# A block of constant matmuls in the stream's form, at 16 operand distances, ahead of a two-block forward pass

## The chip, the cores and the metric

One core of one Trainium2 chip. The metric is the time of one execution on the device, in microseconds (us); lower is better. The inputs are fp32, and so is the output.

## What is computed

The reference runs a sequence of 256 positions of width 1024 through two model blocks of two layers each. Cut to what matters for the work here:

```python
def first_block(x, ...):            # 2 layers
    h = rmsnorm(x, norm_mix_pre[l]); proj = h @ w_in[l]
    # retention, short convolution, 31-tap convolution, three gated branches
    x = x + rmsnorm(merged @ w_o[l], norm_mix_post[l])
    h = rmsnorm(x, norm_ffn_pre[l]); up = causal_dwconv(h @ w_up[l], ffn_conv_w[l])
    x = x + rmsnorm((silu(gate) * val) @ w_down[l], norm_ffn_post[l])

def second_block(x, ...):           # 2 layers
    z = rms(x) @ w_in_2             # mLSTM, sparse attention, differential attention, gates
    x = x + merged @ w_out_2
    x = x + (silu(g) * u) @ w_down_2
```

Nearly all the arithmetic is x times a weight matrix, and every weight is read once.

## The kernel before

The host lays all weight matrices out as one stream of 582 pieces. A piece is 128 partitions x 1024 columns of fp32, 512 KB, eight blocks of 128 x 128, in the order in which TensorE uses them. The activations stand transposed, channels on partitions and the 256 positions along the free dimension.

**A piece's way.** SyncE loads piece j into F[:, j % 5] (`piece`, L2585). ScalarE rounds it to fp32r into H, the high part (`high_part`, L1871). VectorE writes F - H into L, the low part (`low_part`, L1094, its instruction at L1097). The activations are split in the same way, HH and HL (FH and FL for the branch and feed-forward inputs). For every block `channel_blocks` gives TensorE three matmuls of 128 x 256 into one PSUM bank of big: high x high, high weight x low activation, low weight x high activation. Below they are called a triple. All matmuls go through one helper, L582, where the weight (stationary) operand is lhsT and the moving operand is rhs. For v and a few other projections `token_blocks` exchanges the roles: the activation is stationary, and 512 columns of weights move.

```python
mm(ps, hi, xh, start=(k == 0), stop=False)
mm(ps, hi, xl, start=False, stop=False)
r = mm(ps, lo, xh, start=False, stop=last)
```

**Buffers.** F, H and L hold five pieces each. SyncE loads piece j when `low_part` of piece j - 5 is done (s_lo), and ScalarE and VectorE fill H and L of piece j when TensorE has used piece j - 5 (s_mm). They lie in SBUF in the order of their declaration: F, H, L, X, "apart" (48 fp32 columns, 192 bytes, used by nothing), HH, HL, FH, FL, and after them parameters, constants and a pool of tiles called POOL. FHa and FLa are the names of FH and FL as tensors of 14 x 256 columns.

**The order of work.** Each engine has a program of its own, written out as one queue, and semaphores tie them. `tensor_program` walks the groups of the stream. Ahead of the first group it calls `norm(0)`: column sums of the squares of X (L581, helper `column_sums`), a few matmuls of constants to keep the engine busy (`keep_busy`), a matmul with a matrix of ones that spreads the factors over the partitions, and then the first group, four channel groups woven, 32 blocks or four pieces. `norm(0)` on VectorE adds the squares (L1138), forms the factors (L1141 to L1127), prepares the low part of piece 0 and then writes X times factor (L1218) and the low parts of it (L1232); on ScalarE it squares X (L1890), rounds piece 0 (L1874), takes the root (L1867) and rounds the eight tiles to HH (L1907), with the high parts of pieces 1 to 3 between them. VectorE's and GpSimd's queues begin with memsets: two of one element on VectorE (L1815, L1816; ScalarE's first activation waits for the second), four on GpSimd (L2559 to L2562).

**PSUM.** There are eight banks, big0 to big3 for the stream and small0 to small3 for everything else. `norm(0)` uses small0, small2 and small3.

Of the kernel before, what the change touches and what calls it, by code (L numbers as in the profile page):

```python
# [7 lines left out]
F32 = mybir.dt.float32  # L8
# [4 lines left out]
P = 128  # L13
T = 256
# [248 lines left out]
def two_blocks_kernel(nc, stream, params, consts, decay, turn2, lam_rows, xT, head_rows, out):  # L263
# [9 lines left out]
    with ctx:  # L273
        def sb(name, shape, dt=F32):
            return ctx.enter_context(nc.sbuf_tensor(name, shape, dt))

        def sem(name):
            return ctx.enter_context(nc.semaphore(name))

        F = sb("F", [P, NF, PB * P])  # L280
        H = sb("H", [P, NR, PB * P], F32R)
        L = sb("L", [P, NR, PB * P], F32R)
# [4 lines left out]
        FHa = sb("FH", [P, 14, T], F32R)  # L287
        FLa = sb("FL", [P, 14, T], F32R)
# [9 lines left out]
        small = [ctx.enter_context(nc.psum_tensor(f"small{i}", [P, 512], F32)) for i in range(4)]  # L298
# [7 lines left out]
        def tile(i, n=1):  # L306
            return POOL[:, i * T:(i + n) * T]
# [43 lines left out]
        SQ, SK, SV, DQ, DK, DV_, HSQ = 33, 37, 29, 8, 12, 59, 45  # L351
# [42 lines left out]
        s_f = [sem(f"s_f{i}") for i in range(NF)]  # L394
        s_x, s_x2, s_ones, s_par, s_const, s_turn = (sem(n) for n in ("s_x", "s_x2", "s_ones", "s_par", "s_const", "s_turn"))
        s_dec, s_lam, s_out, s_eps, s_pad = (sem(n) for n in ("s_dec", "s_lam", "s_out", "s_eps", "s_pad"))
        s_hi, s_lo, s_mm = sem("s_hi"), sem("s_lo"), sem("s_mm")
        s_eva, s_evd = sem("s_eva"), sem("s_evd")
        s_fill = [sem(f"s_fill{i}") for i in range(4)]
# [120 lines left out]
        def fresh(n):  # L520

            if n == 0 or G[n].layer != G[n - 1].layer:
                return True, 2 * G[n].layer
            if G[n].named("fg"):
                return True, 2 * G[n].layer + 1
            return G[n].named("out") or G[n].named("down"), None
# [34 lines left out]
        def needed(g):  # L561

            m = g.members[0]
            if m.j or m.label not in ("y0", "y1", "y2", "s_k"):
                return []
            if not m.second:
                return {"y0": ["retention"], "y2": ["long_conv"]}.get(m.label, [])
            return {"y0": ["mrows", "mlstm"], "y1": ["choice", *(f"head_{name}" for name in NAMES), "sparse0", "sparse1"],
                    "y2": ["diff0", "diff1"], "s_k": ["ckv"]}[m.label]


        def tensor_program(pe):
# [89 lines left out]
            def channel_blocks(g):  # L662

                n = len(g.members)
                banks_ = [bank_for(m) for m in g.members]
                for i in range(g.nblocks):
                    if i == middle(g):
                        yield
                    k, m, ps = i // n, g.members[i % n], banks_[i % n][:, 0:T]
                    j, o = divmod(g.pos + i, PB)  # L670
                    pe.wait_ge(s_lo, j + 1)
                    hi, lo = H[:, j % NR, o * P:(o + 1) * P], L[:, j % NR, o * P:(o + 1) * P]
                    xh, xl = x_of(m, k)
                    last = k == m.nk - 1
                    wait_x(m, k, False)
                    mm(ps, hi, xh, start=(k == 0), stop=False)
                    wait_x(m, k, True)
                    mm(ps, hi, xl, start=False, stop=False)
                    r = mm(ps, lo, xh, start=False, stop=last)
                    if last or o == PB - 1:  # L680
                        r.then_inc(s_mm, 1)
# [23 lines left out]
            def norm(b):  # L705
                if b == 0:
                    pe.wait_ge(s_ones, 16)
                    bank = use(0, b, "yy")
                    pe.wait_ge(bnd_v.sem, bnd_v.at(b, "add", 0, 6))
                    column_sums(bank, 0, 1, tile(YSQ), True, False)  # L710
                    pe.wait_ge(bnd_v.sem, bnd_v.at(b, "add", 0, 7))
                    column_sums(bank, 0, 1, tile(YSQ + 1), False, True).then_inc(s_fill[0], 1)
                keep_busy(3, 2 if b in SUMMED else 3)
                pe.wait_ge(bnd_v.sem, bnd_v.at(b, "dg"))
                bank = use(2, b, "s1")
                mm(bank[:, 0:T], ones, tile(DG)).then_inc(s_fill[2], 1)
                if b not in SUMMED:
                    keep_busy(3, 4)
                    return
                keep_busy(3, 4)  # L720
                pe.wait_ge(bnd_v.sem, bnd_v.at(b, "dg2"))
                bank = use(3, b, "s2")
                mm(bank[:, 0:T], ones, tile(DG + 1)).then_inc(s_fill[3], 1)
                keep_busy(1, 4)
# [250 lines left out]
            def diff(l, t):  # L975
# [43 lines left out]
                for h in range(4):  # L1019
# [3 lines left out]
                    if h % 2:  # L1023
                        yield

            TASKS = {"retention": retention, "long_conv": long_conv, "choice": choice, "mrows": mrows,
                     "mlstm": mlstm, "ckv": ckv}
            slow = [False]
# [4 lines left out]
            def settle(n):  # L1033

                older = staged.tasks
                staged.tasks = []
                for m in G[n].members:
                    slow[0] = m.label[0:2] == "sc"
                    if m.label == "i_k":
                        staged.begin(m.label, token_weights(m))  # L1040
                    elif m.label in ("out", "down"):
                        staged.begin(m.label, squares(m))
                    for name in begun(m):
                        if name[:-1] in ("sparse", "diff"):
                            beside.add(name, (sparse if name[0] == "s" else diff)(m.l, int(name[-1])))
                        elif name[:5] == "head_":
                            beside.add(name, head(m.l, name[5:]))
                        else:
                            beside.add(name, TASKS[name](m.l))
                newer = staged.tasks  # L1050
                staged.tasks = older
                staged.step()
                staged.tasks += newer

            for n, g in enumerate(G):
                made_after, b = fresh(n)
                if made_after:
                    if n:
                        settle(n - 1)
                    staged.flush()  # L1060
                    if g.layer != G[n - 1].layer:
                        ready.clear()
                    if b is not None:
                        norm(b)
                for name in needed(g):
                    beside.finish(name)
                for _ in token_blocks(g) if g.kind == "t" else channel_blocks(g):
                    if not made_after:
                        settle(n - 1)
                    if paced(n):  # L1070
                        beside.step()
# [5 lines left out]
        def vector_program(dve):  # L1077
            beside, staged = Steps(), Steps()
            v = dve.e
# [12 lines left out]

            def low_part(j):
                dve.wait_ge(s_hi, j + 1)  # L1094
                if j >= NR:
                    dve.wait_ge(s_mm, piece_done[j - NR])
                v.tensor_tensor(L[:, j % NR, :], F[:, j % NF, :], H[:, j % NR, :].bitcast(F32),  # L1097
                                ALU.subtract).then_inc(s_lo, 1)
# [619 lines left out]
            def diff(l, t):  # L1718
# [52 lines left out]
                for k in (2, 3):  # L1771
                    low_branch(2, 2 + l, k, tile(DO + k))

            TASKS = {"retention": retention, "long_conv": long_conv, "choice": choice, "mrows": mrows,
                     "mlstm": mlstm, "ckv": ckv}
# [4 lines left out]
            def settle(n, low=0):  # L1780

                for m in G[n].members:
# [24 lines left out]
                    for name in begun(m):  # L1807
# [4 lines left out]
                        else:  # L1812
                            beside.add(name, TASKS[name](m.l))

            v.memset(eps, EPS)  # L1815
            v.memset(eps64, 64 * EPS).then_inc(s_eps, 1)  # L1816
            for n, g in enumerate(G):
# [33 lines left out]
        def scalar_program(act):  # L1851
# [17 lines left out]

            def high_part(j):  # L1870
                act.wait_ge(s_f[j % NF], 16 * (j // NF + 1))  # L1871
                if j >= NR:
                    act.wait_ge(s_mm, piece_done[j - NR])
                a.activation(H[:, j % NR, :], F[:, j % NF, :], ACT.Copy).then_inc(s_hi, 1)  # L1874
# [451 lines left out]
            def rows_out(l, t, u):  # L2326
# [3 lines left out]

            TASKS = {"retention": retention, "long_conv": long_conv, "choice": choice, "mrows": mrows,
                     "mlstm": mlstm, "ckv": ckv}
# [6 lines left out]
            def settle(n):  # L2339

                for m in G[n].members:
# [27 lines left out]
                    for name in begun(m):  # L2369
# [4 lines left out]
                        else:  # L2374
                            beside.add(name, TASKS[name](m.l))

# [29 lines left out]
        def pool_program(gp):  # L2406
            beside, staged = Steps(), Steps()
            q = gp.e
# [130 lines left out]

            TASKS = {"retention": retention, "long_conv": long_conv, "choice": choice, "mlstm": mlstm, "ckv": ckv}  # L2540

            def settle(n):

                for m in G[n].members:
# [10 lines left out]
                    for name in begun(m):  # L2555
                        if name in TASKS:
                            beside.add(name, TASKS[name](m.l))

            q.memset(glu[:, :, 0:30], 0.0).then_inc(s_pad, 1)  # L2559
            q.memset(tile(CX, 2)[:, 0:2], 0.0).then_inc(s_pad, 1)  # L2560
            q.memset(tile(ROWS), 0.0)
# [245 lines left out]
```

## Time and profile before

| | |
|---|---|
| median of 2 runs | 1868.96 us (1867.89 and 1870.03) |
| profiled execution, from its first to its last instruction | 1870.4 us |
| TensorE busy in it | 1811.5 us, 97% |
| VectorE busy | 1364.4 us, 73% |
| ScalarE busy | 1076.2 us, 58% |
| GpSimd busy | 187.5 us, 10% |
| DMA | 320.08 MB, mean 171 GB/s |

The profiled execution has no time beside its span of its own; the two runs stand for what lies around it, and their median is 1.4 us below that span.

Engines in the rows: PE is TensorE's matmuls, PEld its weight loads, DVE VectorE, ACT ScalarE, POOL GpSimd, SP SyncE. A number such as L582 is a line of the kernel. Matmuls are pipelined and their ends are modelled, so neighbours overlap in the rows: how fast they go is read from the distance between starts. A matmul on plain fp32 operands has two records. PEclk is the clock granted to TensorE, 1.00 being the full one.

### The profile page before, as it was taken

How to read it: one execution, taken by the hardware profiler on the slowest of the kernel's cores; microseconds unless marked ns; L12 is line 12 of the kernel's file. 1: busy time of each engine (PE TensorE's matmuls, PEld its weight loads, DVE VectorE, ACT ScalarE, POOL GpSimd, SP SyncE). 2: the span in 40 equal slices, each digit the busy share in tenths (PEclk: the TensorE clock that was granted, in tenths of full speed). 3: DMA queues.
4: the chain of work that ended last, by engine and by line, in shares of the span. 5: the costliest groups of instructions: out<-in, count | busy, mean ns of one | idle time of the engine just before them, and what ended most of it. 6: DMA issues, size and time to landing. Idle time of an engine off the chain costs nothing.

```text
span 1870.4 us, 36335 instructions
## 1 busy us (share of the span) xinstructions
PE 1811.5 (97%) x14784; PEld 1768.1 (95%) x14784; DVE 1364.4 (73%) x2385; ACT 1076.2 (58%) x1812; POOL 187.5 (10%) x200
## 2 busy tenths in 40 slices
PE   8999999999999999999999999999998999999998
PEld 8899999999899999999889888999998998899998
DVE  6897789867889789866767767655558587676553
ACT  5455656655355666654676685545455757755542
POOL 1012410001003410001111003000002010030000
PEclk9999999999999999999999999999998999999999
DMA  7445536564545536554445644566554375355553
GB/s 283 168 152 187 185 124 203 193 206 155 187 148 180 181 128 200 189 196 135 155 137 167 196 136 129 181 197 193 194 160 140 126 200 160 128 170 180 194 195 108
DMA packets 90342, 320.08 MB, mean 171 GB/s; under 512 B 10528, under 2 KB 12992, under 8 KB 90048
## 3 DMA queue, kind: packets, MB, share of 16 engines
q1 hardware_dynamic: 90176, 317.75, 52.2%
q8 instruction: 118, 1.93, 0.4%
q14 instruction: 48, 0.39, 0.1%
HBM read 310.60 MB, written 1.08 MB: 167 GB/s over the span
## 4 chain that ended last, share of the span: by engine, by line
PE 78%; DVE 11%; ACT 5%; issue 3%; POOL 1%; DMA 1%; SPq 0%; DVEq 0%; ACTq 0%; POOLq 0%
PE big L582 71%; PE small L582 5%; DVE L L1097 3%; PE small L581 2%; DVE POOL L1454 2%; ACT H L1874 2%; DVE POOL L1324 1%; DMA POOL<-POOL 1%; POOL POOL L2470 1%; ACT POOL L2258 1%; DVE gates L1341 0%; DVE POOL L1286 0%; ACT POOL L2296 0%; POOL POOL L2449 0%; SPq L2613 0%
## 5 line engine op out<-in xcount | busy, mean ns | idle before, releaser
L582 PE MATMUL big<-HH,H 128*128 128x256 f32 x3344 | 950.1, 284 | 6.2 <-DVE gates L1341 3.5
L582 PE MATMUL big<-HL,H 128*128 128x256 f32 x3344 | 933.7, 279 | 3.8 <-DVE HL L1232 3.6
L582 PE MATMUL big<-HH,L 128*128 128x256 f32 x3344 | 932.6, 279 | 0.0
L1097 DVE TENSOR_TENSOR L<-F,H 128x1024 fp32r<-128x1024 f32 x574 | 702.4, 1232 | 196.4 <-ACT H L1874 195.0
L1874 ACT ACTIVATE H<-F 128x1024 fp32r<-128x1024 f32 x582 | 610.3, 1054 | 207.5 <-PE big L582 204.4
L582 PEld LDWEIGHTS big<-HH,H 128*128 128x128 f32 x3344 | 634.8, 190 | 11.2 <-DVE gates L1341 4.2
L582 PEld LDWEIGHTS big<-HL,H 128*128 128x128 f32 x3344 | 633.5, 189 | 7.8 <-DVE HL L1232 5.4
L582 PEld LDWEIGHTS big<-HH,L 128*128 128x128 f32 x3344 | 632.6, 189 | 0.0
L582 PE MATMUL big<-FH,H 128*128 128x256 f32 x848 | 240.1, 283 | 0.0
L582 PE MATMUL big<-FL,H 128*128 128x256 f32 x848 | 236.2, 278 | 0.0
L582 PE MATMUL big<-FH,L 128*128 128x256 f32 x848 | 236.1, 278 | 0.0
L582 PEld LDWEIGHTS big<-FH,H 128*128 128x128 f32 x848 | 160.8, 190 | 1.1 <-issue 1.0
L582 PEld LDWEIGHTS big<-FL,H 128*128 128x128 f32 x848 | 159.4, 188 | 1.1 <-issue 1.0
L582 PEld LDWEIGHTS big<-FH,L 128*128 128x128 f32 x848 | 159.3, 188 | 0.0
L582 PE MATMUL small<-POOL 128*128 128x128 f32 (+2 forms) x352 | 82.9, 356 | 26.0 <-DVE POOL L1414 6.8
L1454 DVE SCALAR_TENSOR_TENSOR POOL<-POOL,PR 128x256 f32<-128x256 f32 x240 | 103.9, 496 | 0.1
L582 PE MATMUL big<-ffn,H 128*128 128x256 f32 x512 | 89.2, 277 | 0.0
L582 PEld LDWEIGHTS small<-POOL 128*128 128x128 f32 x352 | 54.1, 194 | 33.6 <-issue 7.7
L582 PEld LDWEIGHTS big<-ffn,H 128*128 128x128 f32 x512 | 77.4, 188 | 0.0
L582 PE MATMUL big<-ffn,L 128*128 128x256 f32 x256 | 71.0, 277 | 0.0
L1355 DVE SCALAR_TENSOR_TENSOR POOL<-big,PR,POOL 128x255 f32<-128x255 f32 x88 | 42.3, 481 | 25.3 <-ACT POOL L2052 20.9
L2449 POOL TENSOR_TENSOR POOL<-POOL,gates 128x256 f32<-128x256 f32 x32 | 30.4, 973 | 266.5 <-DVE gates L1341 266.5
(238 smaller groups left out, 1805.7 us busy)
## 6 DMA issues: line engine op xcount, KB each, us to landing
F<-in_stream SPq DMA_DIRECT2D x582, 512.0 KB, 3.8
POOL<-POOL SPq DMA_DIRECT2D x32, 128.0 KB, 4.2
POOL<-head_rows SPq DMA_DIRECT2D x8, 256.0 KB, 5.0
X<-in_x SPq DMA_DIRECT2D x2, 512.0 KB, 4.4
POOL<-POOL SPq DMA_DIRECT2D x16, 64.0 KB, 3.2
out_x<-X SPq DMA_DIRECT2D x1, 1024.0 KB, 3.9
POOL<-in_decay SPq DMA_DIRECT2D x1, 768.0 KB, 10.9
POOL<-POOL SPq DMA_DIRECT2D x8, 96.0 KB, 5.1
```

What stands on the lines that cost most here:

```text
L581: return pe.e.matmul(out_, lhsT, rhs, start=start, stop=stop, skip_group_check=True)
L582: return pe.e.matmul(out_, lhsT, rhs, start=start, stop=stop)
L1097: v.tensor_tensor(L[:, j % NR, :], F[:, j % NF, :], H[:, j % NR, :].bitcast(F32), ALU.subtract).then_inc(s_lo, 1)
L1324: r = v.scalar_tensor_tensor(out=acc[:, d:T], in0=ps[:, 0:T - d], scalar=par("2m_w", l, (3 - d) * 8 + c), in1=acc[:, d:T], op0=ALU.mult, o ...
L1355: v.scalar_tensor_tensor(out=dst[:, 1:T], in0=ps[:, 0:T - 1], scalar=par("ffn_w", l, 44 + row), in1=dst[:, 1:T], op0=ALU.mult, op1=ALU.add ...
L1454: r = v.scalar_tensor_tensor(out=acc, in0=glu[:, j, k:k + T], scalar=par("cf_w", l, k * 4 + j), in1=acc, op0=ALU.mult, op1=ALU.add)
L1874: a.activation(H[:, j % NR, :], F[:, j % NF, :], ACT.Copy).then_inc(s_hi, 1)
L2258: r = a.activation(p[:, e * nk:(e + 1) * nk], p[:, e * nk:(e + 1) * nk], ACT.Exp, bias=mx[:, e:e + 1], scale=root_of_queries("s_q", qt, pa ...
L2449: q.tensor_tensor(home, home, gate_tile(b, m.j), ALU.add).then_inc(mrg_g.sem, mrg_g.up(m.layer, b, m.j))
L2470: q.tensor_tensor(tile(dst), tile(x), tile(y), ALU.add).then_inc(lc_g.sem, lc_g.up(l, event))
```

## The change

TensorE's queue gets a new function, `warm()`, ahead of the first group's norm. It waits for five memsets (three new ones at the head of VectorE's queue, two at the head of GpSimd's) that fill H and L of slots 3 and 4, one tile of POOL, FH and FL with constants. Then it issues 34 runs of six triples into small2: for 16 starts of the moving operand, 16 bytes apart, the weights being at fixed places, once behind an fp32 matmul of 128 x 256 and once behind an fp32r matmul of 128 x 512 (`pushed`, into small3), and twice more with the order of the triple's last two exchanged. Two runs of six 512-wide matmuls with a 256-wide one behind each (`wide`) close it. No result of these is read. ScalarE's and VectorE's work on piece 3 waits for the block's last matmul (s_warmed), since it overwrites slot 3. Nothing else is changed.

```diff
+        s_warm, s_warmed = sem("s_warm"), sem("s_warmed")
...
+            def warm():
+
+                pe.wait_ge(s_warm, 5)
+                xs, ys = FHa[:, :, :].rearrange("p k n -> p (k n)"), FLa[:, :, :].rearrange("p k n -> p (k n)")
+
+                def pushed(kind):
+                    if kind == 0:
+                        mm(small[3][:, 0:T], tile(HSQ)[:, 0:P], tile(HSQ))
+                    else:
+                        mm(small[3][:, :], H[:, 3, 0:P], H[:, 4, 0:512])
+
+                def triples(n, at, order):
+                    r = None
+                    for k in range(n):
+                        hi, lo = H[:, 3 + k // 8, (k % 8) * P:(k % 8 + 1) * P], L[:, 3 + k // 8, (k % 8) * P:(k % 8 + 1) * P]
+                        xh, xl = xs[:, at + T * k:at + T * (k + 1)], ys[:, at + T * k:at + T * (k + 1)]
+                        turns = ((hi, xh), (hi, xl), (lo, xh)) if order == 0 else ((hi, xh), (lo, xh), (hi, xl))
+                        for i, (w, x) in enumerate(turns):
+                            r = mm(small[2][:, 0:T], w, x, start=(k == 0 and i == 0), stop=(k == n - 1 and i == 2))
+                    return r
+
+                def wide(n, at):
+                    for k in range(n):
+                        hi, lo = H[:, 3, k * P:(k + 1) * P], L[:, 3, k * P:(k + 1) * P]
+                        mm(small[2][:, :], hi, xs[:, at + 512 * k:at + 512 * (k + 1)])
+                        r = mm(small[3][:, 0:T], lo, xs[:, at + 512 * k:at + 512 * k + T])
+                    return r
+
+                for kind in range(2):
+                    for d in range(0, 256, 16):
+                        pushed(kind)
+                        triples(6, (64 + d) % 256 // 4, 0)
+                for kind in range(2):
+                    pushed(kind)
+                    triples(6, 0, 1)
+                    pushed(kind)
+                    r = wide(6, 0)
+                r.then_inc(s_warmed, 1)
...
+            warm()
             for n, g in enumerate(G):
...
             def low_part(j):
                 dve.wait_ge(s_hi, j + 1)
+                if j == 3:
+                    dve.wait_ge(s_warmed, 1)
...
+            v.memset(H[:, 3:5, :].bitcast(F32), 0.5).then_inc(s_warm, 1)
+            v.memset(tile(HSQ), 0.5).then_inc(s_warm, 1)
+            v.memset(FHa[:, :, :].bitcast(F32), 0.75).then_inc(s_warm, 1)
             v.memset(eps, EPS)
             v.memset(eps64, 64 * EPS).then_inc(s_eps, 1)
...
             def high_part(j):
                 act.wait_ge(s_f[j % NF], 16 * (j // NF + 1))
+                if j == 3:
+                    act.wait_ge(s_warmed, 1)
...
+            q.memset(L[:, 3:5, :].bitcast(F32), 0.25).then_inc(s_warm, 1)
+            q.memset(FLa[:, :, :].bitcast(F32), 0.75).then_inc(s_warm, 1)
             q.memset(glu[:, :, 0:30], 0.0).then_inc(s_pad, 1)
```

TensorE's queue before begins with the norm's column sums; small and big are PSUM banks, CO the constants, the names in brackets are semaphores:

```order
L581 MATMUL small<-CO,POOL 128x1 [waits norm_dve,s_ones]
L581 MATMUL small<-CO,POOL 128x1
L581 MATMUL small<-CO,POOL 128x1 [waits norm_dve]
L581 MATMUL small<-CO,POOL 128x1
L582 MATMUL small<-CO 128x128 x3
L582 MATMUL small<-POOL,CO 128x256 [waits norm_dve]
L582 MATMUL small<-CO 128x128 x4
L582 MATMUL big<-HH,H 128x256 [waits x_high,s_lo]
```

In the changed kernel the same queue begins with the block, whose first push waits for s_warm:

```order
L583 MATMUL small<-POOL 128x256 [waits s_warm]
L583 MATMUL small<-FH,H 128x256
L583 MATMUL small<-FL,H 128x256
L583 MATMUL small<-FH,L 128x256
L583 MATMUL small<-FH,H 128x256
```

and goes over from it to the norm, 672 instructions later, thus:

```order
L583 MATMUL small<-FH,H 128x512
L583 MATMUL small<-FH,L 128x256
L582 MATMUL small<-CO,POOL 128x1 [waits norm_dve,s_ones]
L582 MATMUL small<-CO,POOL 128x1
L582 MATMUL small<-CO,POOL 128x1 [waits norm_dve]
L582 MATMUL small<-CO,POOL 128x1
L583 MATMUL small<-CO 128x128 x3
L583 MATMUL small<-POOL,CO 128x256 [waits norm_dve]
L583 MATMUL small<-CO 128x128 x4
L583 MATMUL big<-HH,H 128x256 [waits x_high,s_lo]
```

The norm and the first group stand behind the block in unchanged order, one line number further on.

VectorE's queue in the changed kernel, at its head (SCR holds single columns, eps among them):

```order
L1858 MEMSET H 128x2048
L1859 MEMSET POOL 128x256
L1860 MEMSET FH 128x3584
L1861 MEMSET SCR 128x1
L1862 MEMSET SCR 128x1
L1181 TENSOR_TENSOR POOL<-POOL 128x256 [waits norm_act] x2
```

The three large memsets have come ahead of the two that were there, and of the adds.

## Rows read from the trace of the kernel before

**Rows 1.** The page: busy time by engine, and the chain that ended last

```profile
PE 1811.5 (97%) x14784; PEld 1768.1 (95%) x14784; DVE 1364.4 (73%) x2385; ACT 1076.2 (58%) x1812; POOL 187.5 (10%) x200
...
PE 78%; DVE 11%; ACT 5%; issue 3%; POOL 1%; DMA 1%; SPq 0%; DVEq 0%; ACTq 0%; POOLq 0%
```

**Rows 2.** Timeline of the head: start, length, engine, line, operation, out<-in

```profile
0.87 0.06 DVE L1815 MEMSET SCR<- 128x1 f32 x1 [0.87 <-PEq L2799]
1.21 3.52 POOL L2562 MEMSET POOL<- 128x4096 f32 x1
4.79 2.58 ACT L1890 ACTIVATE POOL<-X 128x256 f32<-128x256 f32 x8 [2.50 <-DMA X<-in_x]
7.76 1.84 PE L581 MATMUL small<-CO,POOL 128*128 128x1 f32 x8 [7.76 <-DVE POOL L1138]
9.46 1.63 PE L582 MATMUL small<-CO 128*128 128x128 f32 x6
10.33 0.42 DVE L1127 TENSOR_TENSOR POOL<-CO,SCR 128x256 f32<-128x256 f32 x1
10.88 1.15 PE L582 MATMUL small<-POOL,CO 128*128 128x256 f32 x2
11.82 1.92 PE L582 MATMUL small<-CO 128*128 128x128 f32 x8
12.07 0.87 DVE L1218 SCALAR_TENSOR_TENSOR POOL<-X,PR,small 128x256 f32<-128x256 f32 x2 [0.18 <-PE small L582]
13.39 0.48 PE L582 MATMUL big<-HH,H 128*128 128x256 f32 x1
13.71 0.28 PE L582 MATMUL big<-HL,H 128*128 128x256 f32 x1
```

**Rows 3.** The chain that ended last, in order of time, in the head

```profile
0.80 3.97 DMA X<-in_x
...
7.76 1.84 PE small L581 x8
...
14.37 1.23 DVE L L1097
...
22.10 0.34 DVE HL L1232
22.44 0.04 issue
22.48 13.79 PE big L582 x119
```

**Rows 4.** Timeline of TensorE in the first group; 17 matmuls lie between the two

```profile
13.95 0.28 PE L582 MATMUL big<-HH,H 128*128 128x256 f32 x1
...
15.99 0.28 PE L582 MATMUL big<-HH,H 128*128 128x256 f32 x1
```

**Rows 5.** The same in a later stretch; 14 matmuls lie between the two

```profile
123.94 0.28 PE L582 MATMUL big<-HH,H 128*128 128x256 f32 x1
...
125.70 0.28 PE L582 MATMUL big<-HH,H 128*128 128x256 f32 x1
```

**Rows 6.** TensorE: 512-wide matmuls, three between the two; then an fp32 pair in the stream

```profile
46.98 0.39 PE L582 MATMUL big<-H,HH 128*128 128x512 f32 x1
...
47.90 0.39 PE L582 MATMUL big<-H,HL 128*128 128x512 f32 x1
...
82.24 0.59 PE L582 MATMUL small<-POOL,CO 128*128 128x256 f32 x2
...
82.90 0.28 PE L582 MATMUL big<-HH,L 128*128 128x256 f32 x1
```

**Rows 7.** TensorE: column sums at a later norm

```profile
242.42 1.39 PE L581 MATMUL small<-CO,POOL 128*128 128x1 f32 x12
```

**Rows 8.** Stretches: length, busy us of each engine, PEclk, DMA share, GB/s

```profile
251.00:256.00 5.00, 3.83 (x22) 3.33 (x22) 4.68 (x13) 1.25 (x4) 2.09 (x3) 0.84 0.31 105
280.00:300.00 20.00, 20.00 (x179) 20.00 (x178) 19.53 (x33) 14.12 (x26) 0.00 (x0) 1.00 0.66 217
```

**Rows 9.** Groups of instructions: the stream's matmuls and their weight loads, busy us, mean ns

```profile
L582 PE MATMUL big<-HH,H 128*128 128x256 f32 x3344 | 950.1, 284 | 6.2 <-DVE gates L1341 3.5
L582 PEld LDWEIGHTS big<-HL,H 128*128 128x128 f32 x3344 | 633.5, 189 | 7.8 <-DVE HL L1232 5.4
```

**Rows 10.** DMA issues: KB each and us from issue to landing

```profile
F<-in_stream SPq DMA_DIRECT2D x582, 512.0 KB, 3.8
```

## The prediction

> **What bounds the kernel now.** I read first the busy shares and the chain that ended last [rows 1]: TensorE is busy 1811.5 of 1870.4 us, 97%, and stands for 78% of the chain. So TensorE's queue is the clock of this kernel, and 1870.4 - 1811.5 = 58.9 us is all that it does not fill. Work put into that queue costs its own length, unless it falls into one of those gaps. Next I read the head in the timeline [rows 2], since the change stands there: TensorE does nothing until 7.76 us, where the column sums of the first norm begin, and the first weight matmul is at 13.39. The chain [rows 3] says what that head hangs on: the load of X, the squares, the sums, and then VectorE and ScalarE, which make the pieces until 22.44; only from 22.48 is it TensorE alone. Last I read the distance from one start to the next in the stream [rows 4 to 6], because a matmul's own duration (284 ns in the mean [rows 9]) overlaps the next and can't be multiplied by a count.
>
> **What the change adds.** warm() stands ahead of norm(0) in TensorE's queue and waits for five memsets. Its count, from the loops: 32 rounds of one push and 6 triples, two more rounds of that kind, and two rounds of one push and 6 pairs of wide and narrow. That is 34 x 18 = 612 matmuls of 128x256 in fp32r, 18 pushes of 128x256 in fp32 (two records each), 18 pushes of 128x512 in fp32r, and 12 x (512 + 256) columns, 672 instructions in all. It moves nothing else; queued behind it on TensorE is everything, and VectorE and ScalarE wait for the norm's sums as before.
>
> **Start of the block.** No VectorE memset of any size is in the trace; the two there are of one element, 0.06 us. The nearest: VectorE's tensor_tensor takes 0.42 us for 256 elements and 1.23 for 1024 [rows 2, 3], so (1.23 - 0.42) / 768 = 1.055 ns an element with 0.15 us fixed. The three memsets write 2048 + 256 + 3584 = 5888 elements: 6.2 us, from 0.87 to about 7.2, and the first push starts near 7.3. Bounds: at GpSimd's rate for a memset, 3.52 us for 4096 [rows 2], it would be 5.1 us and the start near 6.0; at the full 1.23 / 1024 an element 7.1 us and the start near 8.1. I take the slope, since it is this engine's. GpSimd's own two, 5632 elements, take 4.8 us by its row and end near 5.7, so they lie under VectorE's. The eps memset stands behind on VectorE and ScalarE's first activation waits for it, so ScalarE's eight squares (2.6 us) run from about 7.3 to 10; that and VectorE's adds lie under the block and cost nothing. GpSimd's old memset of 4096 ends about 5 us later, also under it.
>
> **Length of the block at the full clock.** The stream starts its 128x256 matmuls 18 in 2.04 us, 0.113 us each, in one stretch [rows 4], and 15 in 1.76 us, 0.117 us each, in another [rows 5]. Stretches of both kinds follow small matmuls in this trace, so I take the middle with a little weight on the slower, 0.1158: 612 x 0.1158 = 70.9 us (bounds 69.2 and 71.8). The wide ones start 0.92 / 4 = 0.23 us apart [rows 6], so 18 x 0.23 = 4.1, and the twelve pairs 12 x (0.23 + 0.115) = 4.1. An fp32 push: from its start at 82.24 to the third matmul behind it at 82.90 is 0.66 us, less two spacings of 0.115 is 0.43 [rows 6]; 18 x 0.43 = 7.8. Together 86.9 us.
>
> **The clock at its start.** The granted clock reads 1.00 over the head, but the durations don't: the same fp32 128x256 pair takes 1.15 us at 10.88 and 0.59 at 82.24, and the pushes of identity columns at 9.46 and 11.82 are as slow [rows 2, 6]. So TensorE ran at 1.2 of its two levels, 1.2 and 2.4 GHz, from its first work at 7.76 until somewhere between 12.03, when that pair ended, and 13.71, the first matmul of 0.28 us. That is 4.3 to 6.0 us after it began to work. The block will begin at the low level too; 5 us at half speed lose 2.5 us (bounds 1.7 and 3.0, and since the slow work of before was sparser, I let it go down to 1.5).
>
> **What comes back.** When the block ends, the clock is high for the norm, and everything it waits for is there. The eight records of column sums took 1.84 us [rows 2]; at the high level twelve take 1.39 [rows 7], so eight take about 1.0: 0.8 back. The sum over all partitions, 1.15 to 0.59: 0.55 back. The rest, from VectorE's first 128x256 at 12.07 to 22.44, is its and ScalarE's chain, equally long after the block: no more comes back, and the small waits of TensorE inside it stay.
>
> **Sum.** 7.3 + 86.9 + 2.5 = 96.7 us is where the column sums begin, against 7.76: +88.9. Less 1.35 is +87.6. The profiled span of 1870.4 becomes 1958.0. The span stands 1.4 us above the median of the two runs, 1868.96, so I predict 1956.6 us. A change under 2%, 37.4 us, counts as none for this kernel.
>
> **Later stages.** Nothing in them is edited. The five pieces in F are loaded while the block runs, yet the pieces behind them need s_lo(0), which comes after the block, and the piece rate is set by TensorE. What can differ is the clock: it falls at the norms and the attention heads, as between 251.0 and 256.0 with 0.84 [rows 8]. Those falls begin at moments that don't belong to the kernel, so 88 us later some will be longer and some shorter; the two runs of before lie 2.1 us apart, and I allow 3 us either way. One of them may now fall on norm(0), since TensorE works thinly there: up to 1.7 us.
>
> **Rival: the distances matter.** The block puts the moving operand at 16 starts, 16 bytes apart, against weights that stand still. In the stream it stands at one of them only, as the declarations have it: H, L and X are multiples of 256 bytes, "apart" adds 192, and HH, HL, FH and FL follow. The token matmuls have the roles exchanged, so 64, and their 512 columns go at 0.23, no slower than two of 256. What speaks for a penalty elsewhere is only that two spacings exist and that a weight load of 189 ns [rows 9] lies beside each matmul of 0.115 spacing, so both operands are read at once. Price: where load and matmul no longer overlap, the spacing can go up to 0.189 + 0.113 = 0.30 us; a distance at which it is bound by the load alone gives 0.189, 0.073 more. If half of the 576 triples' matmuls in the sweep paid that, 288 x 0.073 = 21 us: 1977.6. If a quarter did, 1967. The Trainium skill speaks against it ("TensorE: Matmul & The Clock Gate", step by step, on LDWEIGHTS): the engine has two independent read ports, and loading the next weights takes nothing from the running matmul. By that rule all 16 distances cost alike and the sum above stands; this trace agrees at 192 and 64 and shows no other, and it does show two spacings, which the rule has no name for. Chance of a penalty over 6 us: 0.12.
>
> **Rival: all in the fast spacing, or the memsets quick.** With 0.113 throughout, the block at 6.0 and 1.5 us for the low clock it comes to 6.0 + 85.3 + 1.5 - 7.76 - 1.35 = +83.7: 1952.7. Chance 0.15, inside the range.
>
> **Rival on the other side: the lead pays the block.** Were the stream late because its pieces are late, then a start with F full would take gaps away. Its price: all of the 58.9 us that TensorE does not fill, less the 7.8 of the head, 51.1 us; +87.6 - 51.1 = +36.5, 1905.5, which is not slower by 2%. It decides only if the lead is kept to the end and every gap is a wait for pieces. Against it: a piece of 512 KB lands in 3.8 us [rows 10] and five are in flight, TensorE takes 24 x 0.115 = 2.8 us for one, and the long stretches run without a gap [rows 8]; also the pieces' high parts 3 and up wait for the block, so the lead is five loaded pieces and no more. Chance 0.01.
>
> **Does it do what it says?** If the memsets did not hold TensorE up, or the block lay beside loads that the head waits for, its cost would shrink by at most the 7.76 us of idle head, and that is already in the sum.
>
> **How the numbers follow.** The sum as it stands has 0.72, the fast variant 0.15, the penalty 0.12, the lead 0.01. Terms: start -1.3 to +0.8, spacing -1.7 to +0.9, low clock -1.0 to +0.5, later clock 3 either way, norm(0) up to +1.7. They don't all add on one side, so 1951; above I reach into the penalty case, to 1967. All but the last case lie above 2%: faster 0.005, same 0.015, slower 0.98.
>
> **What would show it.** Right: the first push near 7.3 us, spacings of 0.226 falling to 0.113 to 0.118 some 5 us later, the block's end at 96 to 97, the first matmul on HH and H about 4.3 us behind it, and the stream's groups with the means of before. Wrong: a round of the sweep longer than the others by over 1 us (the distance rival), a first push before 6.5 or after 8.2, or TensorE's idle time without the head far from 51 us.

## The result, and the profile after

| | kernel before | changed kernel |
|---|---|---|
| first measurement | 1868.96 us, 2 runs | 1956.9 us, 2 runs (1950.53 and 1963.27) |
| ratio | | 1.0471, 95% interval 1.0419 to 1.0523 |
| measured again beside the before (e9) | 1869.3 us, 11 runs | 1959.26 us, 6 runs, ratio 1.0471 (1.0427 to 1.0514) |
| profiled execution | span 1870.4 us | 1950.53 us, span 1948.8 us |

Slower by 4.7%, as forecast. The page of the changed kernel has, for [rows 1]:

```profile
PE 1892.5 (97%) x15474; PEld 1845.9 (95%) x15474; DVE 1369.3 (70%) x2388; ACT 1075.8 (55%) x1812; POOL 192.5 (10%) x202
...
PE 80%; DVE 10%; ACT 5%; issue 2%; POOL 1%; DMA 1%; SPq 0%; DVEq 0%; ACTq 0%; POOLq 0%
```

TensorE has 81 us more of busy time, 690 more records (672 instructions, 18 of them with two), and is still 97% busy. Its idle time is 1948.8 - 1892.5 = 56.3 us against 58.9. Without the wait ahead of the first instruction that is 49.2 against 51.1, so next to nothing of the block fell into gaps behind the head.

The head, for [rows 2]; the timeline's columns are start, length, engine, line, operation:

```profile
1.30 1.76 DVE L1858 MEMSET H<- 128x2048 f32 x1 [1.30 <-PEq L2849]
3.06 0.27 DVE L1859 MEMSET POOL<- 128x256 f32 x1
4.03 3.04 DVE L1860 MEMSET FH<- 128x3584 f32 x1 [0.69 <-issue]
7.13 1.22 PE L583 MATMUL small<-POOL 128*128 128x256 f32 x2 [7.13 <-DVE FH L1860]
...
97.15 0.95 PE L582 MATMUL small<-CO,POOL 128*128 128x1 f32 x8
...
99.30 0.70 PE L583 MATMUL small<-POOL,CO 128*128 128x256 f32 x2 [0.43 <-DVE POOL L1170]
...
100.30 0.87 DVE L1261 SCALAR_TENSOR_TENSOR POOL<-X,PR,small 128x256 f32<-128x256 f32 x2
```

The block stands between 7.13 and 97.15, 90.0 us. VectorE's first product of X and the factors, the point from which the head is VectorE's and ScalarE's chain, has moved from 12.07 to 100.30: +88.2 us. What is left to the end took 1848.5 us instead of 1858.3.

What the block itself tells: its rounds. Each begins with a push, so the difference of two pushes is a round of 18 matmuls. Behind the 512-wide push, in the timeline of TensorE:

```profile
61.56 0.39 PE L583 MATMUL small<-H 128*128 128x512 f32 x1
...
63.95 0.39 PE L583 MATMUL small<-H 128*128 128x512 f32 x1
...
66.34 0.39 PE L583 MATMUL small<-H 128*128 128x512 f32 x1
...
68.66 0.39 PE L583 MATMUL small<-H 128*128 128x512 f32 x1
...
71.02 0.39 PE L583 MATMUL small<-H 128*128 128x512 f32 x1
...
73.29 0.39 PE L583 MATMUL small<-H 128*128 128x512 f32 x1
```

These are the rounds at 80 (2.39 us), 96 (2.39), 112 (2.32), 128 (2.36) and 144 (2.27). At 144 every start is 113 or 114 ns behind the one before, from the first; at 112 so from the tenth; at 80 it goes 117, 124, 117, 122 and on, at 96 116, 123, 119, 121 and on, 120 in the mean at both. At 192, the stream's own distance, the round behind the 512-wide push reached 113 after five matmuls, and the one behind the fp32 push stayed at 117 to 119 through all 18. Once settled, all the other rounds at the full clock lie between 116.3 and 120.2 in the mean. So there is a close spacing of 113.3 ns, and there are several wide ones of up to 120; both spacings that the stream showed [rows 4, 5] occur at one and the same distance.

### The profile page after: what moved, and what is told of

Read it like the earlier page. It is cut to its first block, busy times and chain, and to the rows that moved or that the text cites. A ratio compares the mean times of both kernels' runs of the same rounds, so it can differ in the third digit from the quotient of the medians.

```text
span 1948.8 us, 37722 instructions
## 1 busy us (share of the span) xinstructions
PE 1892.5 (97%) x15474; PEld 1845.9 (95%) x15474; DVE 1369.3 (70%) x2388; ACT 1075.8 (55%) x1812; POOL 192.5 (10%) x202
## 4 chain that ended last, share of the span: by engine, by line
PE 80%; DVE 10%; ACT 5%; issue 2%; POOL 1%; DMA 1%; SPq 0%; DVEq 0%; ACTq 0%; POOLq 0%
PE big L583 69%; PE small L583 9%; DVE L L1140 2%; PE small L582 1%; ACT H L1922 1%; DVE POOL L1497 1%; DMA POOL<-POOL 1%; DVE POOL L1367 1%; POOL POOL L2518 1%; ACT POOL L2306 1%; SPq L2663 0%; DVE gates L1384 0%; ACT POOL L2344 0%; PE small L586 0%; POOL POOL L2497 0%
## 5 line engine op out<-in xcount | busy, mean ns | idle before, releaser
L583 PE MATMUL small<-POOL 128*128 128x128 f32 (+2 forms) x388 | 92.9, 356 | 28.1 <-DVE FH L1860 7.1
L583 PEld LDWEIGHTS small<-POOL 128*128 128x128 f32 x388 | 58.9, 191 | 35.6 <-DVE FL L1740 7.3
L583 PE MATMUL small<-FH,H 128*128 128x256 f32 (+1 forms) x216 | 65.6, 306 | 0.0
```

What stands on the lines that cost most here:

```text
L583: return pe.e.matmul(out_, lhsT, rhs, start=start, stop=stop)
```

## Experiments

The kernel before was run beside each group: 19 times with e1 to e4 (median 1872.55 us, 1857.87 to 1884.77), 11 times with e5 to e7 (1873.59), 11 times with e9 and e10 (1869.3). Two questions were open: does the block cost its length and nothing else, and what are the two spacings of the stream?

**e1, the block without its matmuls.** All matmuls but one triple are left out of warm(); the outputs don't depend on it.

```diff
-                for kind in range(2):
-                    for d in range(0, 256, 16):
-                        pushed(kind)
-                        triples(6, (64 + d) % 256 // 4, 0)
...
+                r = triples(1, 0, 0)
                 r.then_inc(s_warmed, 1)
```

> The changed kernel with the block cut to three matmuls (one triple); the five memsets, their waits and the waits on s_warmed stay. Theory (the block costs its own length on TensorE and nothing else): what is left is the delay of VectorE's eps memset, for which ScalarE's squares wait; the squares end about 2.5 us later than before, so 1869 + 2.5 = 1871.5 us, between 1868 and 1875. Rival (the new memsets and waits carry a fixed cost of their own, or the seven more us of lead bring gaps back): outside 1866 to 1876.

Measured: 1868.46 us in 12 runs, ratio 0.9998 (0.9961 to 1.0035). The timeline of its head has the delay that the memsets leave:

```profile
7.14 0.20 ACT L2418 ACTIVATE SCR<-SCR 128x1 f32<-128x1 f32 x1 [5.06 <-DVE SCR L1854]
7.25 2.54 ACT L1930 ACTIVATE POOL<-X 128x256 f32<-128x256 f32 x8
...
10.21 1.84 PE L582 MATMUL small<-CO,POOL 128*128 128x1 f32 x8 [2.07 <-DVE POOL L1173]
```

The column sums begin 2.45 us later than in [rows 2], the 2.5 expected; that is inside the scatter of the runs, so only the profile shows it. Any other cost of the memsets and waits is too small to tell from the runs, whose interval is 0.4%, some 7 us, to either side.

**e2, half the sweep.** The 16 rounds behind the fp32 push are left out.

```diff
-                for kind in range(2):
+                for kind in range(1, 2):
                     for d in range(0, 256, 16):
```

> The changed kernel with the sweep behind the fp32 push left out (16 of the 34 runs of triples); the sweep behind the 512-wide push and the tail stay. Theory (additive): the 16 rounds took 42.6 us in the profile, 1.7 of which is the low clock at the start, which the next rounds inherit, so 40.9 us come back: 1957 - 41 = 1916 us, within 6 us. Rival (part of the cost of the block is fixed, or given back later, because the long dense block changes where the clock falls): more than 8 us off.

Measured: 1918.51 us in 6 runs, ratio 1.0254 (1.0204 to 1.0305). Against 1872.55 the remaining half costs 46 us; 88 - 41 = 47 was due. The cost is additive. Its first rounds:

```profile
7.13 0.79 PE L583 MATMUL small<-H 128*128 128x512 f32 x1 [7.13 <-DVE FH L1860]
...
11.56 0.63 PE L583 MATMUL small<-H 128*128 128x512 f32 x1
...
14.69 0.39 PE L583 MATMUL small<-H 128*128 128x512 f32 x1
```

4.43 and 3.13 us for what takes 2.38 and 2.37 in the changed kernel: here the low clock cost 2.8 us, against 1.7 in the changed kernel's profile (first round 4.25, second 2.57). It is not the missing rounds that do it: e9's profile, of the changed kernel itself, has 4.86 and 3.01 us for the same two, 2.7 us lost. The length of the low clock changes from execution to execution.

**e3, the stream at 112.** No block. HH, HL, FH, FL, ffn and gates are moved so that all the stream's moving operands stand 112 bytes (mod 256) past their weights.

```diff
+        def shifted(name, shape, dt=F32):
+            flat = sb(name, [shape[0], shape[1] * shape[2] + 64], dt)
+            return flat[:, 4:4 + shape[1] * shape[2]].rearrange("p (k n) -> p k n", k=shape[1])
...
-        sb("apart", [P, 48])
-        HH = sb("HH", [P, KT, T], F32R)
-        HL = sb("HL", [P, KT, T], F32R)
+        sb("apart", [P, 24])
+        HH = shifted("HH", [P, KT, T], F32R)
+        HL = shifted("HL", [P, KT, T], F32R)
```

FH, FL, ffn and gates go the same way.

> No block. The kernel before with HH, HL, FH, FL, ffn and gates moved so that every 128x256 matmul of the stream has its moving operand 112 bytes (mod 256) past its weights instead of 192. Theory (the distance decides whether a stretch falls into the spacing of 113 ns): in the sweep the round at 112 reached 113 ns after six matmuls behind both pushes, so the 5,100 stream matmuls that stand at 118 ns drop to 113: about 22 us, 1847 us, and no less than 10 us. Rival (the slow stretches are set by what stands between the matmuls, not by the distance): 1869 within 4 us, and the same 5,100 at 118 ns. Third: 112 locks in only late, and is slower in between: 1869 to 1880.

Measured: 1853.21 us in 8 runs, ratio 0.99 (0.9865 to 0.9935): 1% faster than the kernel before. Of the stream's 13,344 matmuls of 128x256, counted by the distance to the next start, 11,793 stand at 112 to 114 ns and 1,274 at 115 to 129, where the kernel before has 7,953 and 5,109; the rest have a pause behind them. That is 3,835 wide spacings fewer, x 4.5 ns = 17 us, an estimate from one execution of each; the medians differ by 19. e10, with the same layout, has 11,746. The theory was right in its kind and a little too large in its size (22): behind an interruption the stream at 112 needs up to some 15 matmuls before it is at 113.

The spread shrank as well. The eight runs lie between 1847.44 and 1856.37, those of the kernel before between 1857.87 and 1884.77.

**e4, the same distance by the weights.** H and L move by 16 bytes, apart is 128.

```diff
-        H = sb("H", [P, NR, PB * P], F32R)
-        L = sb("L", [P, NR, PB * P], F32R)
+        H = shifted("H", [P, NR, PB * P], F32R)
+        L = shifted("L", [P, NR, PB * P], F32R)
...
-        sb("apart", [P, 48])
+        sb("apart", [P, 32])
```

> No block. The kernel before with H and L moved by 16 bytes and apart made 128 bytes, so that the distance is again 112 mod 256, but the weights and not the moving operand stand off a 32-byte line. Theory (only the distance counts): the same time as the run with the activations moved, within 3 us. Rival (the moving operand's own place counts): 1869 within 4 us whatever the other gives.

Measured: 1914.06 us in 6 runs, ratio 1.0228 (1.0179 to 1.0277). Neither was right: 60 us slower than e3 at the same distance. Only 51 matmuls of the stream stand at 113, the others at 119.6 in the mean. The same stretch as in [rows 8], TensorE only, in e3 and in e4:

```profile
280.00:300.00 20.00, 20.00 (x179) 1.00 0.62 212
```

```profile
280.00:300.00 20.00, 20.00 (x169) 1.00 0.60 201
```

The clock is 1.00 and TensorE 100% busy in both, and yet one gets 179 matmuls done and the other 169: the busy share shows nothing of this, the count does. So the distance is no full description. The buffers' own addresses in the program say where e4 differs: the weights start 16 bytes off a multiple of 32 there, and on one in the kernel before and in e3.

**e5, the stream at 144.** As e3, with apart at 32 columns.

```diff
-        sb("apart", [P, 24])
+        sb("apart", [P, 32])
```

> No block. As the run with the activations at 112, but at 144. In the sweep the round at 144 stood at 113 ns from its first matmul behind the 512-wide push and never reached it (116 to 118) behind the fp32 push. Theory (what stands ahead of a stretch and the distance together decide): stretches behind fp32 matmuls, which are most of the interruptions here, stay at 116 to 118, those behind 512-wide ones at 113; so no gain over 112, and 1860 to 1873 us. Rival (the distance alone decides, and 144 had the shortest round of all): 1850 or less, all at 113.

Measured: 1898.86 us in 6 runs, ratio 1.0142 (1.0107 to 1.0176). The rival falls, and the theory was too kind: 18 matmuls of the stream are at 113, everything else at 118.3 in the mean. The single round of the sweep that stood at 113 at this distance says that the close spacing exists there, not that the stream gets into it.

**e6, long rounds.** 40 triples in a round instead of 6, the operands used over and over, no tail; the outputs don't depend on it.

```diff
-                        hi, lo = H[:, 3 + k // 8, (k % 8) * P:(k % 8 + 1) * P], L[:, 3 + k // 8, (k % 8) * P:(k % 8 + 1) * P]
-                        xh, xl = xs[:, at + T * k:at + T * (k + 1)], ys[:, at + T * k:at + T * (k + 1)]
+                        hi, lo = H[:, 3, (k % 6) * P:(k % 6 + 1) * P], L[:, 3, (k % 6) * P:(k % 6 + 1) * P]
+                        xh, xl = xs[:, at + T * (k % 12):at + T * (k % 12 + 1)], ys[:, at + T * (k % 12):at + T * (k % 12 + 1)]
...
-                        triples(6, (64 + d) % 256 // 4, 0)
+                        r = triples(40, (64 + d) % 256 // 4, 0)
```

> The changed kernel with 40 triples in each of the 32 rounds (six weights and twelve moving tiles used over and over) and no tail. Theory (a stretch at an unfavourable distance never leaves its slow spacing by itself): rounds at 112 and 192 reach 113 ns within some ten matmuls, the others repeat their pattern of 116 to 124 ns for all 120; the kernel takes about 1872 + 3840 x 0.1175 + 16 x 0.43 + 16 x 0.23 = 2334 us. Rival (every stretch reaches 113 in the end, six triples were only too short): all rounds at 113 ns in their last half.

Measured: 2344.72 us in one run. The pushes at 112, 128, and the end of that round, then those at 192 and 208:

```profile
111.65 0.59 PE L583 MATMUL small<-POOL 128*128 128x256 f32 x2
...
125.72 0.59 PE L583 MATMUL small<-POOL 128*128 128x256 f32 x2
...
140.55 0.60 PE L583 MATMUL small<-POOL 128*128 128x256 f32 x2
...
184.23 0.59 PE L583 MATMUL small<-POOL 128*128 128x256 f32 x2
...
198.29 0.59 PE L583 MATMUL small<-POOL 128*128 128x256 f32 x2
```

14.07 us at 112, 14.83 at 128, 14.06 at 192. The last 60 starts of each round are 113.3 ns apart at 112 and 192 behind both pushes, and 116.7 to 120.0 at all other distances. A round that is still wide after its first 18 matmuls stays wide for all 120, and the stream says the same of far longer stretches: in the twelve profiles none changes its spacing later than some 17 matmuls after an interruption, and the longest has 1,582. 144 was wide behind both pushes this time, and 192 close behind both, though it had stayed wide behind the fp32 push in the changed kernel: the first 18 matmuls of a round have the same addresses in both kernels, so at those two distances the same push leads into either spacing, by what ran ahead of it.

**e7, the weights swept.** The moving operand stays at the stream's place, the weights move by 0 to 240 bytes, no tail.

```diff
-                        hi, lo = H[:, 3 + k // 8, (k % 8) * P:(k % 8 + 1) * P], L[:, 3 + k // 8, (k % 8) * P:(k % 8 + 1) * P]
+                        c = 3 * PB * P + off + P * k
+                        hi, lo = hf[:, c:c + P], lf[:, c:c + P]
...
-                        triples(6, (64 + d) % 256 // 4, 0)
+                        r = triples(6, (192 - d) % 256 // 4, 0)
```

> The changed kernel with the moving operand left where the stream has it (192) and the weights moved by 0 to 240 bytes in steps of 16, so that the distances are the same 16, in the same order; no tail. Theory (only the distance counts): each round as long as the one of the same distance in the changed kernel, within 15 ns. Rival (the weights' own place counts beside it: they read slower off a 32-byte line, as the stream at 112 by its weights suggests): the eight odd multiples of 16 stand near 119.6 ns a matmul, 40 ns or more a round above their fellows, the eight even ones equal the changed kernel's rounds.

Measured: 1951.66 us in one run. The eight distances at which the weights start on a multiple of 32 repeat the changed kernel's rounds within 1 ns a matmul at 0, 64, 96 and 224 and within 3 at 32, 128 and 160; 192 is wide behind both pushes, where the changed kernel had it close behind one. Of the eight others none is close. The telling one is 112, close behind both pushes in the changed kernel and 120 behind both here:

```profile
26.85 0.59 PE L583 MATMUL small<-POOL 128*128 128x256 f32 x2
...
29.44 0.59 PE L583 MATMUL small<-POOL 128*128 128x256 f32 x2
```

2.59 us for that round against 2.51 in the changed kernel. "Only the distance counts" falls; the rival's plain 119.6 for all eight is too simple too: they go from 117 to 121, and at 48 and 208 they are shorter than the changed kernel's rounds (2.53 against 2.56 us at 48 behind the fp32 push). In e4 and here only the weights stand off a multiple of 32, the moving operand being on one; both off together was not run.

**e8, a grid.** Weights at 0, 32, ... 224, and for each the moving operand at its 16 places, behind an fp32 push, 14 triples each.

```diff
+                for w in range(0, 256, 32):
+                    for d in range(0, 256, 16):
+                        pushed(0)
+                        r = triples(14, w // 4, (64 + d) % 256 // 4)
```

> The changed kernel with its block replaced by 128 rounds, an fp32 push and 14 triples each: weights moved by 0, 32, ... 224 bytes, and for each of these the moving operand at the 16 places of the sweep. Theory (where the weights stand off a multiple of 32 bytes they only read slower, else the distance counts): for each of the eight places the rounds that end at 113 ns are those whose distance is 112 or 192, so the pattern moves on by two rounds with each step of the weights. Rival (each operand's own place counts, so the distance is no description at all): the rounds at 113 ns are at other distances for other places of the weights, or only where the weights start on a multiple of 128 or 256 bytes. Time: 128 x (0.43 + 42 x 0.118) = 689 us on top of 1872, 2561 us, 20 less or more by how many of them lock.

Measured: 2556.27 us in one run. Mean distance of the last 19 starts of a round, where it was 113.3:

```
weights moved by   0    32    64    96   128   160   192   224
at distance 112   yes   yes   yes   yes   yes   yes   yes   yes
at distance 192   yes   yes   no    yes   yes   yes   yes   yes
elsewhere          -     -     -     -     -    64     -     -
```

The other 112 rounds lie between 116.4 and 120.1. The pushes around the first round of the weights at 64 (distance 192) and around their round at 112, in the timeline:

```profile
181.43 0.59 PE L583 MATMUL small<-POOL 128*128 128x256 f32 x2
...
186.81 0.59 PE L583 MATMUL small<-POOL 128*128 128x256 f32 x2
```

```profile
240.85 0.59 PE L583 MATMUL small<-POOL 128*128 128x256 f32 x2
...
246.10 0.59 PE L583 MATMUL small<-POOL 128*128 128x256 f32 x2
```

5.38 us where it stayed wide, 5.25 where it became close. The rounds at 113.3 move on with the weights, so with weights on a multiple of 32 bytes it is the distance that counts, and the rival of each operand's own place falls. The theory misses one round at 64, and one at 192 that stayed wide; its other half, that weights off such a multiple only read slower, has no round here, and e7 speaks against it.

**e9 and e10, the price once more.** e9 is the changed kernel, e10 the changed kernel with the layout of e3, the block's starts chosen so that its 16 distances are kept.

```diff
-                        triples(6, (64 + d) % 256 // 4, 0)
+                        triples(6, (144 + d) % 256 // 4, 0)
```

> The changed kernel itself, more often, since it has only two runs so far. Theory (the block costs 88.3 us at the full clock and 1.7 for the low clock, less 0.5 for the earlier start and 1.35 in the norm, +88.2 us): ratio 1.047 against the kernel before, 1960 us where that has its median of 1872.5, with the same spread of some 12 us to either side. Rival (the 1957 of the two runs is low because the block spares later falls of the clock): 1952 or less.

> The changed kernel with the activations moved so that the stream stands at 112; the block's own 16 distances are kept by other starts. Theory: the two effects add, 1853 + 88 = 1941 us, and the spread is as small as that of the stream at 112 (within 6 us), so this is the sharper measure of the block's price. Rival (the block leaves TensorE in a state that the stream at 112 profits from or suffers under): more than 5 us off 1941.

Measured: 1959.26 us in 6 runs (1946.77 to 1967.79), ratio 1.0471 (1.0427 to 1.0514), and 1943.98 us in 6 runs (1938.49 to 1946.62), ratio 1.0383 (1.0344 to 1.0421). The effects add: e10 less e3 is 90.8 us, 2.6 more than the theory's 88.2, which two medians of different groups can't tell from it. The rival for e9 falls: no saving in the later stages shows.

## Why the prediction was right

1956.6 us was forecast, 1956.9 measured, 1959.26 in the repeat. The mechanism holds: the block costs its own length on TensorE (e1 and e2), less what the norm gives back. That the median came within 0.3 us is luck: it is that of two runs 12.7 us apart, and the medians of e9 and of e10 less e3 put the cost at 90.0 and 90.8 us, not 87.6. Step by step, by the profile:

- **Start of the block.** 7.3 us forecast, 7.13 measured. From 0.87, where VectorE's first instruction stood before, to 7.07, where the third memset ends, is 6.2 us for 5888 elements, 1.05 ns each: the slope of tensor_tensor was right, without the fixed 0.15 us of each instruction, which the sum left out. The memset rows alone would say 0.86 ns (1.76 us for 2048, 3.04 for 3584), but ahead of these two VectorE stands idle for 0.43 us longer than before and for 0.69 us with nothing that it waits for, and not ahead of the one of 256, at 0.27 us. From 0.87 to the end of the first, and from the end of the second to that of the third, it is 1.07 and 1.04 ns an element. So the rows of the two long memsets most likely begin late; the trace can't prove it.
- **Length.** 86.9 us at the full clock; 90.0 less 1.7 is 88.3. The count was right. The spacing was mis-sized: 116.3 to 120.2 at most of the 16 distances, some 118 over the block, where 115.8, the stream's mixture, was taken; 612 x 2.2 ns is the 1.4 us.
- **The low clock at the start.** 2.5 us forecast, 1.7 in this profile, 2.8 in e2's and 2.7 in e9's.
- **The norm behind it.** The stretch from the column sums to the first product took 3.15 us instead of 4.31: 1.16 back, 1.35 forecast. The clock did not fall there.
- **Together** 88.2 us at the first product, 87.6 forecast: -0.2 for the start, +1.4 for the spacing, -0.8 for the clock, +0.2 for the norm. In e9's profile the product stands at 101.33, +89.3.
- **Later stages.** The profiled run was 9.8 us shorter behind that point than the one of before, more than the 3 allowed. The mean granted clock is 0.992 of 1948.8 us, so 15.6 us were lost, against 0.988 of 1870.4, 22.4 us: up to 7 of the 9.8 are the clock's falls. The two profiles' streams are otherwise alike, 8,031 matmuls at the close spacing and 7,953. e9's runs show that it was this execution and not the change.

The distance rival was wrong in its size: distances do matter, by up to 120.0 - 113.3 = 6.7 ns a matmul, 4 us over the whole block, and not 73 ns. The Trainium skill ("TensorE: Matmul & The Clock Gate", step by step) says that the weight load does not take read bandwidth from the running matmul. The sweep shows a cost that this rule has no place for, 113.3 against 120.0 ns for the same instructions with the moving operand 16 bytes further on (112 and 128, behind the fp32 push); whether it is the reads that collide is not shown. The variant with all of the block at 113 was wrong too, and so was the lead that pays the block: the idle time behind the head went from 51.1 to 49.2 us, not to nothing.

The range was too narrow, and for the wrong reason. It took the scatter of two runs, 2.1 us, and the kernel before scatters over 27 us in all its 44 runs; of the changed kernel's eight runs three lie outside 1951 to 1967. The profiles show where the scatter comes from: in the eight profiles with the stream at 192, 4,009 (e6), 4,249 (e2), 5,801 (e7), 7,374 (e8), 7,953 (before), 8,031 (after), 9,372 (e1) and 9,609 (e9) matmuls are at the close spacing, and at 4.5 ns each the 5,600 between the ends make 25 us. From the first matmul of the stream to the end these profiles take 1866.6 us (e6) to 1841.8 (e1), and the line through the eight falls by 4.3 ns for each further matmul at the close spacing. e2's profiled run, with 4,249, was the slowest of its six, 1929.26 us, and those of e1 and e9 the fastest of theirs. Where a layout leaves no choice, the runs lie closer together: 9 us at 112 (e3), 8 in e10, and 5 and 7.5 in e4 and e5, where all of the stream is wide.

Most of the lot falls in few places. Three stretches of the stream have 1,487, 1,487 and 1,582 matmuls without an interruption, and each is close or wide as a whole once it has settled, worth some 7 us: all close in e1 and e9, two of them wide in e2, e6 and e7, one wide in the others. The first of them, in the changed kernel's two profiles (after, then e9), TensorE only:

```profile
380.00:400.00 20.00, 20.00 (x172) 1.00 0.58 188
```

```profile
380.00:400.00 20.00, 20.00 (x179) 1.00 0.65 210
```

In the block, where TensorE waits for no other engine, these same two executions agree within a nanosecond in every spacing of every round from the sixth on. So the choice at 192 repeats with the same past of TensorE alone, and in the stream something differs from execution to execution ahead of the long stretches. What it is stays open; the kind of push alone doesn't decide it, by e6.

## What to carry to other kernels

- Work put into the queue of an engine that is 97% busy costs its own length: count instructions, multiply by the distance between starts of the same form in the trace, and leave the durations alone. A sweep of this kind is a measurement, and belongs in a kernel of its own.
- In a dense stream of 128x256 fp32r matmuls, each with a weight load of its own, sweep the place of the moving operand against the weights, then test the layout in the stream itself. A stretch of 18 matmuls misleads (144 looked best and cost 1.4%); long stretches behind every kind of interruption tell (112, 1.0% faster, its eight runs within 9 us).
- If single executions of an unchanged program scatter by more than a per cent, count the spacings in several profiles before explaining any of them.

## What the runs showed of the hardware

- TensorE repeats 128x256 fp32r matmuls, each with its own weight load, at 113.3 ns or at a wide pattern of 116.4 to 120.1 ns in the mean, at the same granted clock of 1.00. Which of them depends on the distance of the two operands mod 256 bytes and on what ran before. A stretch settles within its first 15 or so matmuls and then keeps its spacing until it is interrupted (1,582 matmuls in the longest).
- With weights on a multiple of 32 bytes, 112 led into the close spacing in all 8 places of e8 and both rounds each of the changed kernel, e6 and e10. 192 led there mostly. 64 did in one round of e8 and one of e10, 144 in one of the changed kernel and one of e10, all other distances never.
- With weights 16 bytes off a multiple of 32, and the moving operand on one, no round of e7 and no stretch of e4 was close: 119.6 ns through the stream of e4, which was 2.3% slower.
- The granted clock reads 1.00 at the head though the first round took 4.25 us instead of 2.57: the low clock at the start must be read from the durations.
